# Four projection tiles multiplied row by row behind each norm, in a four-layer float32 model on one core

## The reference

```python
def rmsnorm(t, g):
    t32 = t.astype(jnp.float32)
    y = t32 * lax.rsqrt(jnp.mean(t32 * t32, axis=-1, keepdims=True) + EPS)
    return (y * g).astype(t.dtype)

def swiglu(h, w_gu, w_down):
    gate, up = jnp.split(h @ w_gu, 2, axis=-1)
    return (jax.nn.silu(gate) * up) @ w_down

# one layer of the first model; the second has the same frame with other mixers
mod = (c_act @ w_mod[l] + b_mod[l])[:, None, :]
sh1, sc1, g1, sh2, sc2, g2 = jnp.split(mod, 6, axis=-1)
px = (rmsnorm(x, norm1_g[l]) * (1.0 + sc1) + sh1) @ w_in[l] + b_in[l]
...
x = x + g1 * (y_x @ w_out[l])
x = x + g2 * swiglu(rmsnorm(x, norm2_g[l]) * (1.0 + sc2) + sh2, w_gu[l], w_down[l])
```

## Time and profile before

| what | us |
|---|---|
| median of 3 runs | 2379.28 |
| lowest and highest of them | 2376.21, 2380.88 |
| the profiled execution | 2374.06 |
| its span, from the first to the last instruction | 2372.6 |
| TensorE busy | 2217.5 (93%) |
| VectorE busy | 1086.9 (46%) |
| ScalarE busy | 864.2 (36%) |
| mean DMA rate | 130 GB/s |

### The profile page before, as it was taken

The page is one execution under the profiler, slowest core; times in us unless marked ns, Lnnn a source line. Parts: engine busy times, 40 slices in busy tenths (PEclk is TensorE's granted clock), DMA queues, the critical chain, the costliest instruction groups (busy, mean ns, idle before and its releaser), DMA issues.

```text
span 2372.6 us, 28328 instructions
## 1 busy us (share of the span) xinstructions
PE 2217.5 (93%) x11868; PEld 1685.8 (71%) x11868; DVE 1086.9 (46%) x1927; ACT 864.2 (36%) x1324; POOL 0.5 (0%) x6
## 2 busy tenths in 40 slices
PE   4999698999999898799989999899999979998999
PEld 1776476777776776699956447677777757747999
DVE  3383844323232566655554433432322355555555
ACT  2344224222222544544454233422222243354443
POOL 0000000000000000000000000000000000000000
PEclk8999899999999899899999999999999989998999
DMA  9544023454446424356544002345344322202564
GB/s 337 196 150 152 1 71 117 164 160 162 160 132 207 140 89 159 108 167 207 162 145 156 1 1 71 124 163 160 126 155 127 104 72 89 72 1 89 174 201 125
DMA packets 263071, 308.09 MB, mean 130 GB/s; under 512 B 5408, under 2 KB 250272, under 8 KB 250656
## 3 DMA queue, kind: packets, MB, share of 16 engines
q1 hardware_dynamic: 256800, 299.91, 38.4%
q10 hardware_dynamic: 6144, 6.36, 0.8%
HBM read 305.21 MB, written 1.05 MB: 129 GB/s over the span
## 4 chain that ended last, share of the span: by engine, by line
PE 87%; DVE 8%; ACT 3%; issue 1%; ACTq 1%; DMA 0%; DVEq 0%
PE bank L422 86%; DVE yT L1019 2%; DVE input_low L1019 2%; DVE scratch L1019 1%; PE bank L431 1%; ACT L1682 1%; DVE big L1019 1%; ACTq L2089 0%; DMA modulation_slots<-w_mod 0%; ACT yT L1714 0%; DVE big L1423 0%; ACT rstd L1719 0%; DVE xT L1019 0%; ACT rstd L1721 0%; DVE big L1276 0%
## 5 line engine op out<-in xcount | busy, mean ns | idle before, releaser
L422 PE MATMUL bank<-input_high,weights_high 128*128 128x512 f32 (+1 forms) x2336 | 842.6, 361 | 59.6 <-DVE input_low L1019 36.5
L422 PE MATMUL bank<-input_low,weights_high 128*128 128x512 f32 (+1 forms) x2336 | 814.4, 349 | 0.0
L422 PE MATMUL bank<-input_high,weights_low 128*128 128x512 f32 (+1 forms) x2336 | 813.4, 348 | 0.0
L1027 DVE TENSOR_TENSOR weights_low<-weight_slots,weights_high 128x1024 fp32r<-128x1024 f32 (+2 forms) x420 | 453.1, 1120 | 386.4 <-ACT weights_high L1692 385.3
L422 PEld LDWEIGHTS bank<-input_high,weights_high 128*128 128x128 f32 x2336 | 447.0, 191 | 194.7 <-issue 80.3
L422 PEld LDWEIGHTS bank<-input_high,weights_low 128*128 128x128 f32 x2336 | 447.3, 191 | 61.1
L422 PEld LDWEIGHTS bank<-input_low,weights_high 128*128 128x128 f32 x2336 | 448.3, 192 | 58.8 <-issue 4.1
L1692 ACT ACTIVATE weights_high<-weight_slots 128x1024 fp32r<-128x1024 f32 (+2 forms) x420 | 385.4, 966 | 160.9 <-PE bank L422 146.5
L422 PE MATMUL bank<-hidden_high,weights_high 128*128 128x256 f32 (+1 forms) x704 | 242.8, 345 | 0.0
L422 PE MATMUL bank<-hidden_low,weights_high 128*128 128x256 f32 (+1 forms) x704 | 237.4, 337 | 0.0
L422 PE MATMUL bank<-hidden_high,weights_low 128*128 128x256 f32 (+1 forms) x704 | 237.2, 337 | 0.0
(11 more groups left out here) (229 smaller groups left out, 1580.3 us busy)
## 6 DMA issues: line engine op xcount, KB each, us to landing
modulation_slots<-w_mod SPq DMA_DIRECT2D x48, 1024.0 KB, 5.0
modulation_slots<-mod_w SPq DMA_DIRECT2D x48, 1024.0 KB, 4.9
weight_slots<-w_gu SPq DMA_DIRECT2D x44, 1024.0 KB, 5.1
weight_slots<-ffn_w_in SPq DMA_DIRECT2D x44, 1024.0 KB, 5.1
weight_slots<-w_in SPq DMA_DIRECT2D x24, 1024.0 KB, 5.3
weight_slots<-w_down SPq DMA_DIRECT2D x16, 768.0 KB, 5.0
weight_slots<-ffn_w_out SPq DMA_DIRECT2D x16, 768.0 KB, 4.9
...
```

What stands on the lines that cost most here:

```text
L422: return pe.matmul(o, w, r, start=start, stop=stop, skip_group_check=shared)
L1027: tt(m.w_low[:, g % 2, c], m.ring[:, g % SLOTS, c], m.w_high[:, g % 2, c].bitcast(F32), ALU.subtract).then_inc(m.low_made.sem, 1)
```

## The change

Behind each norm the four first tiles are no longer multiplied one after the other. `first_tiles` goes through `FIRST`, a list of pairs (block, row): row 0 of block 0, row 0 of block 1, row 1 of block 0, row 2 of block 0, row 1 of block 1 and so on; at each pair both tiles of the block get their three matmuls, in four PSUM banks. Block 1 is at row k/2 when block 0 is at row k, and its rows 4 to 7 stand at the end. For this the second block must be there early: ACT makes its first half ahead of the last square of the layer part before, DVE behind its last addition to `xT`; the second half is made by ACT behind the first row's piece or pieces, and by DVE within the second row's.

What stood between the four tiles now stands behind them: the modulation steps of these tiles, the sums and swaps of the attention heads in L = 2 and 3, the wait for `odd_set`. In L = 3 the key tiles come ahead of the query tiles (`ODD_TILES`). The load of the Ln and Exp table moves from `rstd` to the start of the output projection and of the second down projection, and those ahead of the attention projections go. At the start ACT issues x and context behind the condition vectors, and SP the eleven tables behind block 1; block 0 now comes ahead of step 7, not of step 2. The diff, cut to its core:

```diff
-ODD_TILES = tuple(8 * part + 2 * i + t for i in range(4) for part in range(3) for t in range(2))
+ODD_TILES = tuple(8 * part + 2 * i + t for i in range(4) for part in (1, 0, 2) for t in range(2))
...
+FIRST = tuple((j, k) for k in range(KD) for j, k in (((0, k), (1, k // 2)) if k % 2 == 0 else ((0, k),))) + tuple(
+    (1, k) for k in range(KD // 2, KD))
...
-                before = g + 6 if g >= 0 else SLOTS
+                before = g + 6 if g >= 0 else 2
...
-    for s in range(SIDES):
+    for s in range(KD - 1):
         step(s)
     weights(0)
-    for s in range(SIDES, KD):
-        step(s)
-    for g in range(1, len(m.item)):
+    step(KD - 1)
+    weights(1)
+    for dst, name in ((m.gate_raw, "p_gate_weights"), (m.lamv[:, 0:4, :], "p_lambda_vectors"), (m.sinks, "p_sinks"),
+                      (m.sgu_wT, "p_sgu_wT"), (m.sgu_bb, "p_sgu_bias_rows"), (m.halves, "k_halves"), (m.swap, "k_swap"),
+                      (m.cos, "k_cos"), (m.sin, "k_sin"), (m.blocked, "k_blocked"), (m.window, "k_window")):
+        sp.dma_start(dst[tuple([slice(None)] * len(dst.shape))], m.A[name]).then_inc(m.tables_in.sem, 16)
+    for g in range(2, len(m.item)):
         for s in m.load_before.get(g, ()):
             step(s)
...
+    def first_tiles(items, n, place, ready):
+
+        for j, k in FIRST:
+            if k in (0, KD // 2):
+                weights(items[j], k // (KD // 2))
+            if j == 0:
+                pe.wait_ge(*ready(k))
+            hi, lo = m.parts(items[j])
+            for t in range(2):
+                c = slice(t * P, (t + 1) * P)
+                i = mm3(bank[place(j, t)][:, 0:n[j]], (hi[:, k, c], lo[:, k, c]), (h_high[:, k, 0:n[j]], h_low[:, k, 0:n[j]]), k == 0,
+                        k == KD - 1)
+                if k == KD - 1:
+                    i.then_inc(m.tile_done.sem, 1)
+
+    def first_projected(L, n):
+        first_tiles(m.proj[L][0:2], n, lambda j, t: 2 * j + t, lambda k: m.norm_low.at(("mix", L), 2 * k + 1))
+        for e in range(4):
+            modulate("proj", L, e)
...
-        if e >= banks:
-            pe.wait_ge(*m.projected.at(L, e - banks))
+        pe.wait_ge(*m.projected.at(L, e - 4 if e in (4, 5) else e - banks))
...
-        for e in range(8):
-            projected_tile(L, e, n, lambda k: m.norm_low.at(("mix", L), 2 * k + 1))
+        first_projected(L, (n, n))
+        if L == 0:
+            pe.wait_ge(*m.tables_in.end(0))
+        for e in range(4, 8):
+            projected_tile(L, e, n)
         pe.wait_ge(*m.gate_w_set.end(L))
...
+        if pairs[0] == 0:
+            first_tiles(m.gu[L, 0], (n, n), lambda j, t: 2 * t + j, lambda k: m.norm_low.at(("ffn", L), per * (k + 1) - 1))
+            for f in range(2):
+                modulate("hidden", L, f)
         for p in pairs:
+            if p == 0:
+                continue
...
-        for e in range(14):
+        first_projected(L, (TOK, TOK))
+        even_head_sums(0)
+        even_tokens(0)
+        for e in range(4, 14):
             if e < 12:
-                projected_tile(L, e, TOK, lambda k: m.norm_low.at(("mix", L), 2 * k + 1), 2)
-            if e in (2, 4):
-                even_tokens(e // 2 - 1)
-            if 1 <= e and e - 1 in EVEN_NORMED:
+                projected_tile(L, e, TOK, 2)
+            if e == 4:
+                even_swap(0)
+                even_head_sums(1)
+                even_tokens(1)
+                even_swap(1)
+            if 5 <= e and e - 1 in EVEN_NORMED:
                 even_head_sums(EVEN_NORMED.index(e - 1))
-            if 2 <= e and e - 2 in EVEN_NORMED:
+            if 6 <= e and e - 2 in EVEN_NORMED:
...
-            projected_tile(L, e, SEQ if ODD_TILES[e] < 8 else TOK, lambda k: m.norm_low.at(("mix", L), 2 * k + 1), 2)
-            if e:
-                if e - 1 in ODD_NORMED:
-                    odd_head_sums(ODD_NORMED.index(e - 1))
-                else:
-                    odd_tokens(ODD_TILES[e - 1] - 16)
-            if 2 <= e and e - 2 in ODD_NORMED:
+        first_projected(L, (TOK, SEQ))
+        odd_head_sums(0)
+        odd_head_sums(1)
+        pe.wait_ge(*m.odd_set.end(0))
+        for e in range(4, 24):
+            projected_tile(L, e, SEQ if ODD_TILES[e] < 8 else TOK, 2)
+            if e == 4:
+                odd_swap(0)
+                odd_head_sums(2)
+                odd_swap(1)
+            elif e == 5:
+                odd_head_sums(3)
+                odd_swap(2)
+                odd_tokens(0)
+            elif e - 1 in ODD_NORMED:
+                odd_head_sums(ODD_NORMED.index(e - 1))
+            else:
+                odd_tokens(ODD_TILES[e - 1] - 16)
+            if e == 6:
+                odd_swap(3)
+                odd_scores(0)
+            elif 8 <= e and e - 2 in ODD_NORMED:
                 odd_swap(ODD_NORMED.index(e - 2))
...
     def odd_mixer(L):
-        pe.wait_ge(*m.odd_set.end(0))
         odd_projection(L)
...
+    def coming_weights(L, e):
+        if e in (0, 2):
+            next_weights(m.proj[L][1 + e // 2])
+        elif e >= 6 and e % 2 == 0:
+            next_weights(m.proj[L][e // 2])
...
+            if i == 2 * per - 1:
+                low_weights(second, range(1, 2))
...
+        low_weights(m.gu[L, 0][1], range(1))
...
+        if part and L < 3:
+            low_weights(m.proj[L + 1][1], range(1))
...
     def rstd(place, t, b=7):
-        ln_exp_tables()
         act.wait_ge(*m.square_added.end(place))
         F(rs[:, t], bank[b][:, t], ACT.Ln, bias=m.eps[:, :]).then_inc(m.root.sem, 1)
         act.wait_ge(*m.root.at(place, 0))
         F(rs[:, t], rs[:, t], ACT.Exp, scale=-0.5).then_inc(m.root.sem, 1)
...
+            if i == per - 1:
+                high_weights(second, range(1, 2))
...
         n = N_OUT[L]
+        ln_exp_tables()
         for e in range(KD):
             if e % 2 == 0:
                 next_weights(m.outp[L][e // 2])
+            if e == KD - 1:
+                high_weights(m.gu[L, 0][1], range(1))
...
+        if part and L < 3:
+            ln_exp_tables()
         for f in range(KD):
             next_weights(m.down[L, part][f])
+            if f == KD - 1 and part and L < 3:
+                high_weights(m.proj[L + 1][1], range(1))
...
-    for t, src in ((xT[:, :, X], "p_x"), (xT[:, :, C], "p_ctx")):
-        act.dma_start(t, m.A[src]).then_inc(m.input_in.sem, 16)
-    for dst, name in ((m.gate_raw, "p_gate_weights"), (m.sgu_wT, "p_sgu_wT"), (m.sgu_bb, "p_sgu_bias_rows"), (m.sinks, "p_sinks"),
-                      (m.halves, "k_halves"), (m.swap, "k_swap"), (m.cos, "k_cos"), (m.sin, "k_sin"),
-                      (m.blocked, "k_blocked"), (m.window, "k_window")):
-        act.dma_start(dst[tuple([slice(None)] * len(dst.shape))], m.A[name]).then_inc(m.tables_in.sem, 16)
-    act.dma_start(m.lamv[:, 0:4, :], m.A["p_lambda_vectors"]).then_inc(m.tables_in.sem, 16)
     act.wait_ge(*m.columns_in.end(0))
     act.wait_ge(*m.consts.at(0, 5))
     condition(0)
+    for t, src in ((xT[:, :, X], "p_x"), (xT[:, :, C], "p_ctx")):
+        act.dma_start(t, m.A[src]).then_inc(m.input_in.sem, 16)
+    ln_exp_tables()
     rstd("first", slice(0, TOK))
     high_weights(0)
     modulate("start", KD - 1)
+    high_weights(1, range(1))
     for L in range(2):```

The order of the instructions that the program holds shows where the modulation steps of mix 2 went. The stretch is on TensorE; `modulation_slots` is a modulation step (x4 is one step), `mean_over_head_halves` the sum of a head's squares, `input_` by `weights_` a projection. Before, at the end of the second tile of mix 2:

```order
L422 MATMUL bank<-input_high,weights_high 128x512
L422 MATMUL bank<-input_low,weights_high 128x512
L422 MATMUL bank<-input_high,weights_low 128x512
L422 MATMUL bank<-modulation_slots,condition_vectors 32x512 x4
L422 MATMUL bank<-yT,mean_over_head_halves 128x512
L422 MATMUL bank<-input_high,weights_high 128x512
```

84 lines of the change are left out of this document (39 added, 45 removed).

## The result

| kernel | median us (lowest to highest) | ratio to before, 95% interval |
|---|---|---|
| before, 5 runs beside it | 2376.21 (2375.20 to 2380.88) | |
| changed, 5 runs | 2364.89 (2361.87 to 2365.82) | 0.9949 (0.9936 to 0.9962) |

The account below looks back on a forecast made before the run. TensorE, busy 93% of the span, was taken as the bound, through its idle stretches and low clock. Terms -3.8 - 3.7 - 4.0 - 3.6 - 2.0 - 6.5 + 2.9 + 1.4 = -19.3 us gave 2360, range 2346 to 2371.

Parts of the forecast that it names:

- The four of the network and mix 1: Norm stages' forecast changes: ffn 0 -3.8, ffn 1 -3.6, ffn 2 -3.7, ffn 3 -2.0, mix 1 -4.0 us.
- TensorE is bound by its own work from the first row on: ffn 0's first four tiles: 2.1 us of matmuls per 1.6 us row; 22.4 work, 1.8 low clock, 2.1 modulation steps.
- Mix 3: L = 3's norm: fifth tile 11.1 us earlier without the early odd_set wait, part given back by later waits; -6.5 us taken.
- The modulation steps: Mix 0 and mix 2: steps in a row stall for loads, 2 us clock loss per stall; +1.4 and +2.9 us.
- the landing row: Profile row giving 4.98 us for a modulation load to land; the prediction used it over the skill's 4.4 us estimate.
- Table loads: Removing Ln/Exp table loads in front of 1/root: 0 gain, except in front of mix 2, -2.1 us.
- If the loads behind them shift along, step 7 lands at 34: Start: condition vectors come some 9 us earlier, so modulation step 7 lands at 34, not 42.6; norm starts at 46.2.
- The rule of the two slots: Modulation loads: SP may load step s only when step s - 2 is multiplied; a load takes 4.98 us.
- Rival 1: Mix 0 and mix 2: loads land in time, no stalls; gain 33 us, 2346 us; chance 0.12.
- Rival 2: Behind the four tiles: TensorE waits 1.5 us in each of eight places; gain 7, 2372 us; chance 0.14.
- Rival 3: Four tiles at 512 wide stay at 1.2 GHz in ffn 0, ffn 2, mix 0, mix 2; 2428 us; chance 0.03.
- Rival 4: Rows stay the limit in each norm because extra half blocks stop DVE and ACT; no change, 2379; chance 0.03.

Follow-up runs that it names:

- tile_by_tile: The changed kernel with the four first tiles of every norm multiplied tile by tile, all else as changed: 2400.59 us, ratio 1.0099.
- The odd_set wait alone: The kernel before with one edit: in mix 3 TensorE's wait for odd_set stands in front of the fifth tile, not the first: 2372.55 us, ratio 0.9979.
- squares_early: The changed kernel with the first norm's sums of squares behind modulation steps 2 to 5 instead of 4 to 7: 2358.27 us, ratio 0.9921.
- x_first: The changed kernel with squares_early's edit and x and context loaded on ScalarE ahead of its wait for the parameter columns: 2354.08 us, ratio 0.9898.

## Why the prediction was right, and where it was off

The time fell in the range and the mechanisms named did act, but the gain of 11.3 us is 8 short of the forecast and just under its own bounds of 12 to 28. That 2364.89 lies only 4.9 off the 2360 is in part luck: the kernel before ran 3.1 us under its earlier median of 2379.28 in this sitting.

**The norms.** The four of the network and mix 1 were put at -17.1 together and gave -16.6. The step "TensorE is bound by its own work from the first row on" held: 22.4 + 1.8 + 2.1 = 26.3 for ffn 0, and 26.1 came. tile_by_tile shows that the order does it. (The 44 matmuls in 10 us of the earlier trace rows count two that the edges cut; start to start is 0.233 us.) In mix 1 I had the fifth tile at 809.9, and it came at 809.89 in the trace, which is luck: all was 0.9 us late by then, so the stretch won 4.9 and not 4.0. Another 0.9 came behind the later stall of 4.43 us, where TensorE was at half clock for 3.4 us instead of 6.8. In ffn 1 the stretch took 12.7 us where I had 12.3, but its first row came 1.6 us late against the level in front of the norm, nearly all of it because the last sums of squares ran at half clock.

**Mix 3.** -6.5 forecast, -6.0 measured, by larger parts: -12.6 and +6.6 instead of -11.1 and +4.6. The wait of the second scores is 1.45 as forecast, that of the second swap 0.70 instead of 1.9. What I did not have are three waits of 0.65, 0.66 and 0.68 us in front of turns of values at 1968, 2008 and 2048 (above), each for DVE's rotation. That is 2.0 us, which the kernel before lacks and the second profile of the changed kernel has again (0.69, 0.68, 0.69). The odd_set wait alone gives 4.1.

**The modulation steps.** The mechanism was right and shown: 4.58, 4.25 and 0.55 us of stall against 3.9, 3.9 and 1.8 forecast. Of the clock I had charged 2 us behind each. In mix 0 3.4 us at half speed lost 1.7; in mix 2 it was 10.2 us, 8.0 of them with work, so 4.0 lost, twice the forecast. The second swap's wait there was 1.79 against 1.9. The Trainium skill (DMA: Bandwidth & Descriptors, Anatomy of one DMA — SWDGE (gpsimd) path) fits 2.0 us plus the bytes at 436 GB/s to DMAs issued by GpSimd, an estimate of 4.4 us for such a load. Here SP issues them, and the 96 loads of the changed kernel took 4.7 us at the least and 5.1 in the median, so the landing row was the better guide.

**Table loads.** 0.1 here and there and -2.1 in mix 2 were forecast; the loads put back cost 0.1, and 2.76 in front of mix 2, less the 0.5 for the half block. The Trainium skill (ScalarE: Activation LUTs, What ACT_TABLE_LOAD costs) puts a switch to another table at about twice the load itself, by the drain it adds. The trace disagrees: in front of mix 2 two loads cost 2.76 us, which is 2 x 1.28 and 0.2. In the changed kernel's second down projection of L = 1, where the table changes from that of Silu, the load stands 0.02 us behind the instruction before it (1158.36 to 1158.38), and the next starts 0.01 us behind its end (1159.67).

What I had put at nothing is the loads' new place. In that down projection, ahead of mix 2, ACT loads the table at 1158.38 and makes the high part of a block behind it; DVE waits 1.63 us for that part where before it waited 0.20, and TensorE then 0.45 for `weights_low`. In the output projection of L = 3 the load at 2143.40 does the same (DVE 2.02 instead of 0.59), and TensorE waits 0.58 us for a square at 2149. The kernel before has neither of these waits of TensorE, and the second profile of the changed kernel has both (0.45 and 0.54).

**What failed: "If the loads behind them shift along, step 7 lands at 34".** It landed at 40.1. Behind it the sum was right: 12 us to the norm were forecast, and 12.1 came. With 34 I would have put the norm at 46.2; it started at 52.23. From the first step to step 7 the kernel before took 23.5 us and the changed one 29.5, so the loads did not just shift. Before, x, context and block 0 had all landed by 18.65, while TensorE still waited for the condition vectors. Now these three megabytes stand among the steps. Context landed at 23.8, and step 2 took 7.83 us where before it took 4.91. Block 0 landed at 37.6, and step 7 took 6.79 where before it took 4.98. Besides, the squares that had covered the loads of steps 3 to 6 now stand behind steps 4 to 7, and steps 3 and 4 are waited for by 1.02 and 2.25 us. The rule of the two slots holds at the start in both kernels, so each longer load delays the one two steps on. By the stages the start costs 5.5 of the 10.1 us between the forecast and the difference of the profiles. squares_early and x_first show the parts: both edits together bring the first row 7.4 us sooner, 4.6 of them by x alone. Block 0's share is less clear, since moving it up helped step 7 and held up step 5.

**Most of the rest of the miss is the clock, by place.** Mix 2 was 3.4 us worse than forecast. From 1185 to 1245 the granted clock was 0.91 before and 0.80 after, and squares_early in its first profile had that stage 5.9 us better with the same code. The mLSTMs, which the change does not touch, moved by -2.0 and +2.2. The low stretches add up to 147 us before and 140 after. Where rows or the wait for `odd_set` had left gaps, the clock came back as they closed: 0.53 before and 0.81 after from 790 to 808 in mix 1, 0.62 and 0.90 from 1903 to 1920 in mix 3, the same in both profiles of the changed kernel. In ffn 0 it stayed at 0.76.

**The rivals.** Rival 1 (steps cost nothing) is out by the stalls. Rival 2 (given back behind the tiles) shows as 0.66 us in mix 1 and nothing in ffn 0. Rival 3 did not happen: the granted clock around ffn 0 was 0.76 over 14 us, as before. Rival 4 is out by the stretches from first row to fifth tile. The range held the time.
